# Holding GpSimd's weight splits back until the last token tile of a normalising boundary is scaled

## The reference, cut to what matters

```python
for i in range(DEPTH):                       # DEPTH = 2
    m = _even_mixer(...) if i % 2 == 0 else _odd_mixer(...)
    x = _layer_norm(DN_ALPHA * x + m, ln1_g[i], ln1_b[i])
    x = _layer_norm(DN_ALPHA * x + _sq_relu_mlp(x, w_up[i], w_down[i]), ln2_g[i], ln2_b[i])
    gate = jax.nn.sigmoid(x @ ple_w_gate[i] + ple_b_gate[i])
    x = x + gate * (p[i] @ ple_w_proj[i])
...
x = x + mixed                                # third layer
h2 = rmsnorm(x, norm2_g)
x = x + (silu(h2 @ w_ffn_gate) * (h2 @ w_ffn_up)) @ w_ffn_down
return rmsnorm(x, norm_f_g)
```

## Time and profile before

| what | us |
|---|---|
| median of three runs | 2122.43 |
| the profiled execution | 2123.25 |
| its span, first to last instruction | 2121.4 |
| PE busy | 1991.2 |
| POOL busy | 1246.2 |
| DVE busy | 922.5 |
| ACT busy | 317.5 |

### The profile page before, as it was taken

One profiled execution on the slowest core, in us unless ns is written; L12 is line 12 of the kernel. 1 busy time (PEld: TensorE's weight loads), 2 busy tenths in 40 slices (PEclk: granted clock), 3 DMA queues, 4 the chain that ended last, 5 costly groups with the idle time before them and its releaser, 6 DMA issues.

```text
span 2121.4 us, 24646 instructions
## 1 busy us (share of the span) xinstructions
PE 1991.2 (94%) x9028; PEld 1645.2 (78%) x9028; DVE 922.5 (43%) x1321; ACT 317.5 (15%) x612; POOL 1246.2 (59%) x719
## 2 busy tenths in 40 slices
PE   7888889999997999999999999988898989999998
PEld 7667778888886778787778888876687778888886
DVE  2479463243338511378262253356647951000234
ACT  1046230000003100156110000020321121000001
POOL 5475356667775455643466667756453365666675
PEclk9989999999999999789999999999998999999999
DMA  5310123332332222211233333232221122233322
GB/s 202 119 40 1 60 70 119 99 92 96 99 98 90 70 90 85 70 32 43 81 108 94 94 99 99 92 107 70 73 80 60 50 85 94 91 97 99 96 92 79
DMA packets 53404, 181.23 MB, mean 85 GB/s; under 512 B 6552, under 2 KB 9290, under 8 KB 53210
## 3 DMA queue, kind: packets, MB, share of 16 engines
q1 hardware_dynamic: 46512, 165.17, 24.5%
q10 hardware_dynamic: 6826, 15.11, 2.1%
HBM read 176.56 MB, written 3.70 MB: 85 GB/s over the span
## 4 chain that ended last, share of the span: by engine, by line
PE 80%; DVE 12%; ACT 2%; POOL 2%; issue 2%; DMA 0%; POOLq 0%; DVEq 0%; ACTq 0%
PE PS L577 77%; PE PS L721 2%; DVE PB L1252 1%; DVE X L1360 1%; POOL WL L482 1%; PE PS L770 1%; ACT PTH L1750 1%; DVE PTL L1258 1%; DVE X L1361 1%; POOL WH L479 1%; DVE X L1322 1%; DVE STL L1594 1%; DVE X L1422 0%; DVE XTL L1351 0%; DVE X L1305 0%
## 5 line engine op out<-in xcount | busy, mean ns | idle before, releaser
L479 POOL TENSOR_SCALAR WH<-RW 128x1024 fp32r<-128x1024 f32 x303 | 362.6, 1197 | 730.3 <-PE PS L577 691.4
L482 POOL TENSOR_TENSOR WL<-RW,WH 128x1024 fp32r<-128x1024 f32 x303 | 772.0, 2548 | 25.2
L577 PE MATMUL PS<-XTH,WH 128*128 128x512 f32 x1168 | 463.4, 397 | 16.4 <-ACT HT L1801 11.8
L577 PE MATMUL PS<-XTL,WH 128*128 128x512 f32 x1168 | 459.8, 394 | 0.0
L577 PE MATMUL PS<-XTH,WL 128*128 128x512 f32 x1168 | 459.4, 393 | 0.0
L577 PEld LDWEIGHTS PS<-XTH,WH 128*128 128x128 f32 x1168 | 222.9, 191 | 66.8 <-ACT HT L1801 13.2
L577 PE MATMUL PS<-WL,HSH 128*128 128x512 f32 x688 | 267.6, 390 | 2.1 <-POOL WL L482 2.1
L577 PE MATMUL PS<-WH,HSH 128*128 128x512 f32 x688 | 267.7, 389 | 0.0
L577 PE MATMUL PS<-WH,HSL 128*128 128x512 f32 x688 | 267.7, 389 | 0.0
L577 PEld LDWEIGHTS PS<-XTH,WL 128*128 128x128 f32 x1168 | 222.3, 190 | 47.7
L577 PEld LDWEIGHTS PS<-XTL,WH 128*128 128x128 f32 x1168 | 222.9, 191 | 45.0
(11 more groups left out here) (314 smaller groups left out, 2364.0 us busy)
## 6 DMA issues: line engine op xcount, KB each, us to landing
RW<-stream SPq DMA_DIRECT2D x303, 512.0 KB, 3.5
BC<-gate_rows SPq DMA_DIRECT2D x16, 256.0 KB, 3.2
G<-gain_rows ACTq DMA_DIRECT2D x5, 512.0 KB, 3.6
XS<-xt ACTq DMA_DIRECT2D x4, 512.0 KB, 7.9
X<-x ACTq DMA_DIRECT2D x1, 2048.0 KB, 11.0
G<-bias_vecs ACTq DMA_DIRECT2D x4, 512.0 KB, 4.9
out<-X SPq DMA_DIRECT2D x4, 512.0 KB, 2.6
bias_rows<-QM ACTq DMA_DIRECT2D x1, 1536.0 KB, 6.9
```

What stands on the lines that cost most here:

```text
L479: pool.tensor_scalar(WH[:, j % WS, :], RW[:, j % RAW, :], 1.0, 1.0, ALU.mult, ALU.mult).then_inc(hi_split, 1)
L482: pool.tensor_tensor(WL[:, j % WS, :], RW[:, j % RAW, :], WH[:, j % WS, :].bitcast(F32), ALU.subtract).then_inc(lo_split, 1)
L577: return pe.matmul(o, a, b, start=start, stop=stop)
```

## The change

`cut_from(a, first, b, n)` makes POOL's cuts from chunk a up to the first chunk of stage `first`, waits until `last_centred` has been raised n + 1 times, and makes the cuts from there to b. The two long runs of cuts are divided with it at up0, ple0, up1, ple1 and ffn, the stages behind the boundaries b = 0, 1, 3, 4 and 6. The cuts, their order and all other engines' lists stay as they are. The boundaries ahead of fox and gla (b = 2, 5) get no wait.

```diff
+            def cut_from(a, first, b, n):
+
+                over_chunks(pool, a, FIRST[first], cut)
+                pool.wait_ge(last_centred, n + 1)
+                over_chunks(pool, FIRST[first], b, cut)
+
...
-            over_chunks(pool, FIRST["out0"] + WS - 1, FIRST["out1"] + WS - 1, cut)
+            cut_from(FIRST["out0"] + WS - 1, "up0", FIRST["ple0"], 0)
+            cut_from(FIRST["ple0"], "ple0", FIRST["out1"] + WS - 1, 1)
...
-            over_chunks(pool, FIRST["out1"] + WS - 1, CHUNKS, cut)
+            cut_from(FIRST["out1"] + WS - 1, "up1", FIRST["ple1"], 2)
+            cut_from(FIRST["ple1"], "ple1", FIRST["ffn"], 3)
+            cut_from(FIRST["ffn"], "ffn", CHUNKS, 5)
```

## The result

The median of the changed kernel is 2147.18 us (four executions: 2137.03, 2147.17, 2147.19, 2147.85), against 2121.72 us for the kernel before, run beside it: a ratio of 1.0118 with a 95% interval of 1.0094 to 1.0141. It is slower, as forecast, but by 25 us where 13 were forecast, and outside the range of 2129 to 2142.

A forecast was written before the change was run, and what follows sets the result against it. DVE's chain of scalings and splits, taking turns with POOL's cuts, was taken to bound PE at the boundaries; 12.6 us net plus 0.5 for the clock gave 13.1, so 2135.5 us against the median 2122.4, range 2129 to 2142 (8 in 10).

The forecast's parts named there:

- What bounds, and how the engines meet: At the boundaries PE waits for DVE's list, where two scalings beside POOL's cuts take 2.68 and 1.35 us instead of 0.81.
- the rule of turns: DVE and POOL on SBUF: while one has its instruction under way the other stands; whichever queued first is served first.
- The gain: Last scaling at five boundaries ends earlier, no longer waiting for POOL: 1.12 to 1.35 us each, sum 6.2 us.
- The price: POOL's cuts fall on DVE's first splits; PE starts 8.15 us after the last scaling's end (z): +12.6 us net over five boundaries.
- The clock at the starts: PE's longer standstill ahead of the stages lowers its clock: half a microsecond more at b = 3, bounds -1.5 and +5.
- rival 3: Starts at b = 0, 3 and 6 stay at 1.2 GHz twice as long, 1.7 us each: 2138 to 2142 us, chance 8%.
- What moves with it: Behind the boundaries, later steps shift with PE's start and DVE keeps its phase to POOL's cuts; nothing added or absorbed.
- The sign: Whole kernel slower: 0.6% forecast, with chance 0.82 of being slower by over 0.2%.

The follow-up runs named there:

- held_apart: Changed kernel, with POOL's second cut behind each of the five boundaries also waiting until DVE has split two feature tiles: median 2131.1 us, ratio 1.0044 to the kernel before.
- warm_gla: Changed kernel plus seven extra PE matmuls between the last transposes of b = 5 and gla's first matmul: median 2138.7 us, ratio 1.0079 to the kernel before.
- pool_gla: Changed kernel, with POOL's cut of gla's chunk 20 waiting until DVE has normalised and gated the second token tile's output: median 2142.9 us, ratio 1.0098 to before.
- only_ple1: Changed kernel with only one of its five waits kept, that behind b = 4: median 2123.8 us, ratio 1.0021 to the kernel before.
- only_ffn: Changed kernel with only one of its five waits kept, that behind b = 6: median 2123.8 us, ratio 1.0004 to the kernel before.
- gaps_three: As in_gaps, but only behind b = 0, 3 and 6, with the old order behind b = 1 and 4: median 2123.6 us, ratio 1.0007 to before.
- second_held: As held_apart without the wait for the last scaling: POOL's first cut early, second after two splits; median 2135.5 us, ratio 1.0063 to the kernel before.
- in_gaps: Changed kernel with the four POOL instructions of each boundary's first two cuts spread over gaps in DVE's port use: median 2114.3 us, ratio 0.9964 to before.

## Why the prediction was wrong, point by point

**What bounds, and how the engines meet: right.** The chain through DVE's list and the rule of turns held instruction by instruction. The rule quoted from the Trainium skill (SBUF — State Buffer, Who interferes with whom), that the order of issue decides who blocks, agrees with this case's trace: POOL's WH was issued at 656.56 and the cast at 656.91, and the cast ended last.

**The gain: right.** 1.28 us was worked out for b = 1. In the changed kernel the last scaling ends 11.25 us after the first addition (641.43 to 652.68), before it was 12.48 (639.63 to 652.11): 1.23.

**The price: right, size and kind.** PE was to start at z + 8.15; at b = 1 it starts at 660.91 - 652.68 = z + 8.23. POOL began at z + 0.44, where I took 0.25. For the five boundaries I had 2.26, 3.09, 2.54, 2.41, 2.34, sum 12.6; measured 2.36, 3.22, 2.64, 2.51, 2.40, sum 13.1. held_apart shows that it is the second cut that costs it.

**The clock at the starts: near in sum, not in its parts.** 0.5 us was taken, all of it for b = 3; the stages other than gla lost 0.9 in sum. Up1 and down1 lost 0.24. Ple0 and ple1, where the wait for EL was to hide the loss, lost 0.85 and 0.79, and ffn won 1.17. All five stages now begin with a matmul of 0.76 or 0.77 us, at 1.2 GHz, where two did, as rival 3 had it. But its price wasn't paid: over the first ten microseconds the mean clock fell from 0.83 to between 0.72 and 0.78 in four stages and rose from 0.72 to 0.84 in ffn.

**What moves with it: this step failed.** It said that behind a boundary everything shifts together, that DVE's meetings with POOL's cuts keep their phase, and closed with "So the delay stays and isn't absorbed". I had looked at up, down and ple, where that is so (0 to 0.85 us), and took it for all. Gla is different. Its PE, DVE and POOL steps wait for each other in both directions, and its start depends on the clock. The stage began at 1.2 GHz, lost 2.9 us on its first chunk (POOL's next cut at 8.8 instead of 5.9 us after the start), and later came to its second output tile with POOL's cut 1.3 us earlier against DVE. The cut then fell on four DVE instructions and made them 3 us longer, one tile sooner than such a meeting comes in the kernel before, and the steps paired off differently to the end of the stage: one wait of 5.41 us more, and a lower clock. The term for this stage stood at nothing and measured 11.2 us. warm_gla takes away the first link and 10.4 us; pool_gla takes away the second and 8.4 (the second follows from the first, so the two don't add). That the delayed boundary makes the start slow is shown only as a frequency: by their times three to five of only_ple1's ten executions have it, the kernel before in none of its three profiles of that start (before, only_ffn and gaps_three have no edit at b = 4, and all begin gla at a full clock). Nor is a late boundary needed for it: second_held has the slow start with b = 4 shorter than before, and held_apart and in_gaps, which change b = 4 as well, begin at 1.00 in their profiles. What sets the clock of a start that lies 80 us behind the edit isn't settled; PE's long gaps just ahead of it (5.7 and 2.4 us) are the same in both cases.

**The range** was made of errors inside the terms that I had: tails of the turns, POOL's start, clock at three starts. Each of these was small, and no term stood for a stage that comes out otherwise. Twelve microseconds more at the upper end would have been the price of one sentence on gla. The sign came out as forecast, and the price of the boundaries alone, 13 us, gives it. Of the rivals, none happened as priced. Rival 3 named the clock, but its 1.7 us at each of up0, up1 and ffn aren't in the stages (up0 to down0 and up1 to down1 +0.24 together, ffn -1.17).

## What to carry to other kernels

When two engines take turns on a port, moving work out of one gap moves it into the next: list every gap of the other engine, with its length, and place the work by instruction; four instructions of 1.05, 1.05, 2.35 and 2.35 us placed so gave 8.0 us at the boundaries, where moving them as a block cost 13.1. Then look at what the last of them meets further on: here it took back 4.9 of the 8.0. Ahead of predicting that a delay only shifts what follows, look for a stage in which engines wait for each other in both directions and PE has gaps: there a shift of 1.3 us cost 8 here. Compare the stages one by one, since a sum over all of them mixes the edit's own effect with lengths that vary by 7 and 11 us.

## What the runs showed of the hardware that was not expected

- The same stage with the same instructions has two lengths, 225 and 236 us (gla to out2), and fox to out1 takes between 311.7 and 318.8. They go with stretches at 1.2 GHz: 0.55 against 0.65 of full speed over 34 us of fox, and 0.92 against 0.95 over gla, which has one wait of PE of 5.41 us more in its long form.
- Seven matmuls that compute nothing, 1.9 us of work in a gap, made the changed kernel around 9 us shorter (2148.1 to 2138.7 in the medians), since the stage behind began at 2.4 GHz. The Trainium skill (TensorE: Matmul & The Clock Gate, What's actually happening) has the array's clock follow how busy it was; the granted clock of 1.00 against 0.69 in the first ten microseconds agrees.
- Four DVE instructions of 128x128 with two SBUF inputs took 1.14 us alone and 4.16 beside one POOL cut of 3.5 us. The first ended at 1665.62, just behind POOL's WH (1665.48), the second at 1668.12, just behind its WL (1667.97; the recorded starts of these two, 1665.55 and 1665.57, are too close to tell who asked first), and the last two were free: one short instruction got in between POOL's two, and the row as a whole stood behind both.
